# Gate products of tile pairs as seven half-size block products in a two-layer block on one Trainium2 core

## The reference

```python
p = h @ w_in[l]                       # h: 512 token rows (and, in layer one, 256 context rows) x 1024
o_a = global_attention(...)           # 512 features each
o_b = window_attention(...)
o_c = short_conv(...)
g_a, g_b, g_c = jnp.split(jax.nn.sigmoid(p[..., OFF_GATE:]), 3, axis=-1)     # 1024 features each
merged = g_a * (o_a @ w_branch[0]) + g_b * (o_b @ w_branch[1]) + g_c * (o_c @ w_branch[2])
x = x + gt1 * (merged @ w_out)
```

## Time and profile before

| | |
|---|---|
| median of three runs | 3093.0 us (3089.81 to 3094.14) |
| profiled execution | 3090.21 us, span 3088.4 us |
| PE busy | 2977.6 us, 96% of the span |
| DVE, ACT busy | 1051.9 us (34%), 613.1 us (20%) |
| layer one's merge | about 436 to 870 us of the span |
| layer two's merge | about 1895 to 2172 us |
| granted PE clock, mean | 0.995 |

### The profile page before, as it was taken

One profiled execution on the slowest core, in us unless ns is written; L12 is line 12 of the kernel. 1 busy time (PEld: TensorE's weight loads), 2 busy tenths in 40 slices (PEclk: granted clock), 3 DMA queues, 4 the chain that ended last, 5 costly groups with the idle time before them and its releaser, 6 DMA issues.

```text
span 3088.4 us, 32609 instructions
## 1 busy us (share of the span) xinstructions
PE 2977.6 (96%) x13043; PEld 1402.2 (45%) x13043; DVE 1051.9 (34%) x1566; ACT 613.1 (20%) x1121; POOL 75.0 (2%) x88
## 2 busy tenths in 40 slices
PE   7999999999999999999999999999979898899999
PEld 4565655555545222222335555444323222244547
DVE  4754645556514000000157553011120010137352
ACT  3135530000003110111031552000111100021161
POOL 1000000000000010102000000000000000000000
PEclk9999999999999999999999999999999999999999
DMA  8120013534513999999850101222499999963200
GB/s 253 41 83 14 15 52 124 185 137 146 174 41 143 388 369 401 365 401 357 314 157 14 56 20 53 77 67 95 177 355 408 408 408 408 407 206 82 68 1 28
DMA packets 266076, 578.83 MB, mean 187 GB/s; under 512 B 62040, under 2 KB 140136, under 8 KB 265800
## 3 DMA queue, kind: packets, MB, share of 16 engines
q1 hardware_dynamic: 258064, 554.09, 48.9%
q0 software_dynamic: 7552, 22.61, 2.4%
q10 hardware_dynamic: 312, 0.05, 0.0%
HBM read 561.49 MB, written 15.20 MB: 187 GB/s over the span
## 4 chain that ended last, share of the span: by engine, by line
PE 87%; DMA 9%; DVE 2%; issue 1%; ACT 1%; SPq 0%; DVEq 0%; POOL 0%; ACTq 0%; POOLq 0%
PE ps L1026 32%; PE ps L1430 10%; PE ps L1545 6%; PE ps L1042 5%; PE ps L1442 5%; PE ps L1090 5%; PE ps L1258 4%; PE ps L1270 3%; PE ps L1304 3%; PE ps L1103 3%; DMA ring<-in_w_e_down 2%; PE ps L1066 2%; PE ps L1486 2%; DMA ring<-in_w_e_gate 1%; DMA ring<-in_w_e_up 1%; PE ps L1240 1%
## 5 line engine op out<-in xcount | busy, mean ns | idle before, releaser
L1026 PE MATMUL ps<-hT,ring 128*128 128x512 f32 (+1 forms) x2080 | 771.8, 528 | 1.5 <-ACT hT L1772 1.4
L1026 PEld LDWEIGHTS ps<-hT,ring 128*128 128x128 f32 x2080 | 394.4, 190 | 366.1 <-issue 341.7
L1430 PE MATMUL ps<-ring,hT 128*64 128x512 f32 x992 | 234.4, 602 | 3.8 <-DMA ring<-in_w_e_up 3.8
L1042 PE MATMUL ps<-hT,ring 128*128 128x512 f32 (+1 forms) x448 | 181.5, 533 | 0.7 <-DVEq L1757 0.7
L1772 ACT ACTIVATE prob<-ps 128x512 f32<-128x512 f32 (+1 forms) x67 | 46.4, 692 | 681.0 <-PE ps L1026 681.0
L1545 PE MATMUL ps<-ring,hT 128*64 128x512 f32 x640 | 150.4, 603 | 14.9 <-DMA ring<-in_w_e_down 10.6
L1772 ACT ACTIVATE prob<-prob,nms 128x768 f32<-128x768 f32 (+5 forms) x224 | 159.2, 711 | 18.9 <-DVE nms L2395 8.6
L1090 PE MATMUL ps<-merged,ring 128*128 128x512 f32 (+1 forms) x384 | 144.4, 531 | 3.1 <-issue 3.1
L1026 PE MATMUL ps<-obuf,ring 128*128 128x512 f32 (+1 forms) x384 | 143.4, 523 | 0.0
L1270 PE MATMUL ps<-con,prob 128*128 128x128 f32 x872 | 140.2, 283 | 1.3 <-DVE merged L2419 0.5
L1270 PEld LDWEIGHTS ps<-con,prob 128*128 128x128 f32 x872 | 96.4, 140 | 89.5 <-issue 78.8
(11 more groups left out here) (341 smaller groups left out, 3204.0 us busy)
## 6 DMA issues: line engine op xcount, KB each, us to landing
ring<-in_w_e_gate SPq DMA_DIRECT2D x79, 1024.0 KB, 15.8
ring<-in_w_e_up SPq DMA_DIRECT2D x65, 1024.0 KB, 15.0
ring<-in_w_e_down SPq DMA_DIRECT2D x60, 1024.0 KB, 14.6
ring<-in_w_in SPq DMA_DIRECT2D x49, 1024.0 KB, 6.9
ring<-in_w_ada SPq DMA_DIRECT2D x48, 1024.0 KB, 6.8
merged<-in_w_e_up SPq DMA_DIRECT2D x25, 1024.0 KB
merged<-in_w_e_down SPq DMA_DIRECT2D x19, 1024.0 KB
merged<-in_w_e_gate SPq DMA_DIRECT2D x18, 1024.0 KB
```

Of the source, the lines that this page charges most:

```text
L1026: mm = pe.matmul(ps[:, b + a:b + e], lhs[:, k, :], rhs[:, k, a:e], start=k == 0, stop=k == nk - 1)
L1042: mm = pe.matmul(ps[:, BANK[SIDE]:BANK[SIDE] + hi - lo], ring3(slot)[:, k, m % 2 * P:(m % 2 + 1) * P], h3[:, k, lo:hi], start=k == 0, stop ...
L1430: mm = pe.matmul(ps[e * CX:(e + 1) * CX, b + h * 512:b + (h + 1) * 512], lhs, second_weights(slot_of[sub], e, h), start=k == 0, stop=k == ...
```

## The change

For a pair of tiles (256 gate features) the 1024x256 weight chunk and the 1024x512 token columns are each cut in 2 x 2 blocks: two halves of K (0:4, 4:8), two feature tiles, two halves of 256 token columns. The four output blocks come from seven block products (a Strassen-Winograd scheme) in place of eight. All twelve pairs of layer two are done so, and the eight pairs of branches 0 and 1 in layer one; layer one's branch 2 stays as it was, and context columns are multiplied plainly (`context`).

New jobs: `hsum` (DVE: sums of token blocks, once per layer, in place in `h3` too), `wsum` (DVE: sums of weight blocks, one per pair, placed ahead of the branch jobs of the pair before), `gate2` (PE: `seven_products`; ACT and DVE: copy, additions, sigmoids).

```diff
+            def long(j):
+                return {"hsum": 0, "wsum": 0, "gate2": 2}.get(j[0], 1)
...
-            count, passed, share = len(todo), 0, len(jobs) - 4
+            count, passed, share = len(todo), 0, sum(map(long, jobs)) - 4
...
+                if j[0] in ("hsum", "gate2") or j[0] == "branch" and j[2] < 2 and j[3] % 2:
+                    continue
                 while todo and (count - len(todo)) * share < passed * count:
...
+            in_pairs = ((0, 1), (2, 0, 1))[l]
+            pairs = [(l, br, n) for br in in_pairs for n in range(KD // 2)]
...
+            dense += [j for p in pairs[:1] for j in (("hsum", l), ("wsum",) + p)]
+            for at, p in enumerate(pairs):
+                dense += [("gate2",) + p] + [("wsum",) + q for q in pairs[at + 1:at + 2]]
+                dense += [("branch", l, p[1], 2 * p[2] + m) for m in range(2)]
...
+                if j[1:] == PAIR_FIRST[l]:
+                    need(oT_ready, ("O", l, 2 * TILES[l] - 1))
+                    need(token_sums_ready, ("hsum", l))
...
+                times("p1", a, w[:, 0:4, 0:P], h3[:, 0:4, 0:HALF], True)
+                if l == 0:
+                    context(0)
+                need(weight_sums_ready, ("wsum",) + j[1:])
+                times("p6", b, s2, t2, True)
+                times("p5", c, s1, t1, True)
+                if l == 0:
+                    context(1)
+                need(seven_added, j[1:] + ("u2",))
+                times("p7", b, s3, h3[:, 0:4, HALF:NX], False)
+                need(first_product, j[1:])
+                times("p2", a, w[:, 4:8, 0:P], h3[:, 4:8, 0:HALF], False)
+                need(seven_added, j[1:] + ("u3",))
+                times("p4", b, w[:, 4:8, P:2 * P], t4, False)
+                need(seven_added, j[1:] + ("22",))
+                times("p3", c, s4, h3[:, 4:8, HALF:NX], False)
+                chunk_end[cn] = (seven_full.sem, seven_full.at[j[1:] + ("p3",)])
...
+                elif kind == "gate2":
+                    b = BANK[job[j][0]]
+                    if before_pair[j[1:]][1]:
+                        A.need(gate_used, before_pair[j[1:]][1])
+                    A.need(seven_full, j[1:] + ("p1",))
+                    A.do(sc.copy(probT[:, 1, 0:HALF], ps[:, b:b + HALF]), first_product, j[1:])
...
+                    V.do(v.tensor_tensor(t1, b12, b11, ALU.subtract))
+                    V.do(v.tensor_tensor(t2, b22, t1, ALU.subtract))
+                    V.do(v.tensor_tensor(t4, b21, t2, ALU.subtract))
+                    V.do(v.tensor_tensor(b12, b22, b12, ALU.subtract), token_sums_ready, j)
...
+                    if before_pair[j[1:]][0]:
+                        V.need(seven_full, before_pair[j[1:]][0][1:] + ("p3",))
...
+                    V.do(v.tensor_tensor(s1, a21, a22, ALU.add))
+                    V.do(v.tensor_tensor(s2, s1, a11, ALU.subtract))
+                    V.do(v.tensor_tensor(s4, a12, s2, ALU.subtract))
+                    V.do(v.tensor_tensor(s3, a11, a21, ALU.subtract), weight_sums_ready, j)
...
+                    V.need(first_product, j[1:])
+                    V.need(seven_full, j[1:] + ("p6",))
+                    V.do(v.tensor_tensor(c12, p1, second, ALU.add), seven_added, j[1:] + ("u2",))
+                    V.need(seven_full, j[1:] + ("p7",))
+                    V.do(v.tensor_tensor(c22, p1, second, ALU.add), seven_added, j[1:] + ("u3",))
+                    V.do(v.tensor_tensor(c22, c22, third, ALU.add), seven_added, j[1:] + ("22",))
```

More of the change, by code:

```diff
@@ L790, in chunk_of @@
                 return (kind, l, t // 2), t % 2
+            if kind in ("gate2", "wsum"):
+                return ("gate", l, t, j[3]), 0
             if kind == "gate":
@@ L830, in chunk_dmas @@
             return plain(w_out[l], n * CH)
-        WEIGHTED = ("qk", "v", "conv_c", "conv_x", "conv_b", "gate", "branch", "silg", "side", "wout", "wt")
+        WEIGHTED = ("qk", "v", "conv_c", "conv_x", "conv_b", "gate", "gate2", "wsum", "branch", "silg", "side", "wout", "wt")
         def chunk_keys(j):
@@ L1027, in product, with seven_products, times, context @@
                 part(mm, key)
+            def seven_products(j):
+                l = j[1]
+                cn, slot = weights(chunk_of(j)[0])
+                if j[1:] == PAIR_FIRST[l]:
+                    need(oT_ready, ("O", l, 2 * TILES[l] - 1))
+                    need(token_sums_ready, ("hsum", l))
+                a = begin(j)
+                b = a + 512
+                c = begin(j + ("c",), HEAD_SUMS if l == 0 or j[3] % 2 else SIDE)
+                w = ring3(slot)
+                s1, s2, s4, s3 = weight_sums
+                t1, t2, t4 = token_sums[l]
+                def times(name, bank, lhs, rhs, first):
+                    for k in range(4):
+                        mm = pe.matmul(ps[:, bank:bank + HALF], lhs[:, k, :], rhs[:, k, :],
+                                       start=first and k == 0, stop=k == 3, skip_group_check=not first)
+                    mm.then_inc(seven_full.sem, 1)
+                def context(m):
+                    if m == 0:
+                        begin(j + ("x",), SIDE)
+                    o = BANK[SIDE] + m * NC
+                    for k in range(KD):
+                        mm = pe.matmul(ps[:, o:o + NC], w[:, k, m * P:(m + 1) * P], h3[:, k, NX:NT], start=k == 0, stop=k == KD - 1)
+                    if m == 1:
+                        part(mm, j + ("x",))
+                times("p1", a, w[:, 0:4, 0:P], h3[:, 0:4, 0:HALF], True)
[15 more added lines that the diff above has]
+                chunk_end[cn] = (seven_full.sem, seven_full.at[j[1:] + ("p3",)])
             def run(j):
@@ L2300, in run @@
                     g = probT[:, d % 2, 0:w]
-                    V.need(sig_ready, ("gate", l, br, d))
+                    if (l, br, d // 2) in before_pair:
+                        V.need(pair_sigmoid, (l, br, d // 2, "12"))
+                    else:
+                        V.need(sig_ready, ("gate", l, br, d))
                     b = V.read(j)
```

63 lines of the change are left out of this document (59 added, 4 removed).

## The result

The changed kernel takes 3171.7 us (median of 4 runs, 3170.8 to 3175.8) against 3092.1 us (4 runs) for the one before on the same chip: ratio 1.0263, 95% interval 1.0251 to 1.0276. It is 80 us slower; the forecast was 3146 us, with a range of 3126 to 3162. The direction was right, the size missed by 26 us.

The account below looks back on a forecast made before the run. PE was taken to bound both merges, with SP's queue stalling layer one after the change. Layer one +58, clock +10 and layer two -13.5 gave +55 on 3090.2, 3145, stated as 3146 us for the median; range 3126 to 3162.

Parts of the forecast that it names:

- layer one without clock: From layer one's last branch-2 product to its last branch product: 321.0 us against 262.8 before, +58.2.
- low clock, both layers: Lower PE clock behind seven stalls in layer one and one in layer two: 10 us of at most 16.
- layer two without clock: Layer two's 12 pairs: 20.6 us saved, 7.1 us of waits for `hsum` and `wsum` at the start, -13.5.
- stretch between the merges: From layer one's merge to layer two's: no change, since nothing behind the merges absorbs the difference.
- Bound, gain, mechanism: In both merges PE binds; twenty pairs save 34.3 us without waits; layer one's late branch chunks in SP's queue decide.
- Landing ... 2.5 MB land after 9.3, 3.5 MB after 11.9: Layer one's branch chunks behind `w_ada` chunks: PE idle 9.4 us at pairs 1, 2, 5 and 12.0 at 3, 4, 6.
- A stall costs between 0 and 2.0 us more ... I take 10 us: Clock price behind eight stalls, seven in layer one and one in layer two: 10 us taken of at most 16.
- The row for 2.0: Earlier trace: after 12.13 us idle PE runs at 0.50, eight 0.43 us instructions take 5.46, 2.0 us lost.
- The row for 0: Earlier trace, program's start: after 9.24 us idle the clock shows 1.00, read as no loss.
- Products: Both merges: seven products of a pair take 12.00 us, 1.714 each; with layer one's context products 18.86.
- The first, 3108: Rival: layer one's transfers hide and DVE's queue binds, layer one +27 instead of +58, total 3108 us; chance 0.08.
- Worse than the sum: Rival: stalls at the upper landing, all with low clock, 0.25 us more per pair: 3160 us and over; chance 0.12.

Follow-up runs that it names:

- e3: Changed kernel with plain products instead of the seven in layer one's branches 0 and 1, new order of jobs and chunks kept, layer two unchanged: 3169.6 us.
- e1: Changed kernel with each layer-one pair's 0.5 MB branch chunk read directly behind that pair's gate chunk, ahead of the `w_ada` chunks: 3133.0 us.
- e10: Changed kernel with layer one's branch chunk (branches 0 and 1) in one transfer of 128 partitions instead of two of 64: 3165.0 us.
- e6: Changed kernel, but SP issues nothing behind a branch chunk of layer one's branches 0 and 1 until that chunk has landed: 3171.8 us.
- e9: Changed kernel with PE multiplying constants in six layer-one stalls, fills cut to the measured waits: 3161.8 us.
- e2: Changed kernel with seven products in layer two alone; layer one's merge has the earlier kernel's job order and plain products: 3078.6 us.
- e13: Changed kernel with the turn of the three PSUM slots moved on by two ahead of layer one's first w_out product: 3171.9 us.
- e8: Changed kernel with branch chunk ahead, `w_ada` sums moved, layer one's first-pair context products before the sums, three of layer two's `hsum` instructions early: 3085.8 us.
- e5: Changed kernel with PE multiplying 20 to 31 products of constants before the first branch product of six layer-one pairs: 3232.8 us.

## Why the prediction was right in direction and wrong in size

The 80.6 us between the two spans, by the terms of my sum:

| term | forecast | measured |
|---|---|---|
| layer one without clock | +58.2 | +69.6 |
| low clock, both layers | +10 | +21.8 |
| layer two without clock | -13.5 | -13.6 |
| stretch between the merges | 0 | +3.5 |
| rest | 0 | -0.7 |

So the sum was 26 us short: 11.4 in layer one's landings and products, 11.8 in the clock, 3.5 in the stretch between, and 0.8 the other way.

- **Bound, gain, mechanism: right.** Six stalls for `in_w_branch` of 8.8 to 12.7 us, `hsum` 10.7 (forecast 10.4) and 6.1 (5.9), u2 2.0 (2.3), pair 7 2.1. e3 shows that the order of jobs and chunks alone makes the loss, and e1 that 39 us of it hang on the place of the branch chunk. Layer two is right to 0.1 us.
- **"Landing ... 2.5 MB land after 9.3, 3.5 MB after 11.9": too short.** From the end of p3 to PE's start it was 10.5 to 11.8 us at pairs 1, 2 and 5 and 13.4 to 13.7 at the others; with pair 7 the stops sum to 78.4 us where I had 68.4. I scaled the branch chunk's 1.3 us from its size, and it comes in two transfers of 64 partitions: in one, a wait is 1.4 us shorter (e10), and at pair 2 PE starts 9.35 us after the first issue (718.82 to 728.17), where I had 9.4. The Trainium skill's fit (DMA: Bandwidth & Descriptors, Anatomy of one DMA) was for the other path; the estimate by it, 8 us for 2.5 MB, misses the measured 10.2 (e6) by 2.2 us, my own by 0.9.
- **"A stall costs between 0 and 2.0 us more ... I take 10 us": neither end was a bound.** Here 1.5 to 3.1 us were lost behind each of the seven branch stalls (14.4 in all), 2.8 behind each `hsum`, and 1.8 behind the 1.99 us wait for u2: 21.8 us. I had counted eight stalls; pair 7's and u2's short waits make ten. e9 gives 9.9 of it back. Both rows that I read the earlier trace rows say less than I took from them.

  The row for 2.0: the clock was low from PE's return at 2256.27 to about 2261.8. Of these 5.5 us the first 2.0 passed over four products of 16 columns and 0.91 us of idle, so only 3.6 us of low clock fell on dense work. The eight instructions were not all at 0.50 either: at 0.86 us each they would have taken 6.9 us, not 5.46.

```profile
2260.00:2262.00 2.00, 2.00 (x4) 0.88 (x3) 0.00 (x0) 0.00 (x0) 0.96 (x1) 0.55 0.68 158
```

  The row for 0: the clock column says 1.00 at the program's start, but the 42 equal instructions there did not run at one pace. PE was busy throughout, and the first 24 took 5.0 us (0.21 each), the rest about 0.11 each. The windows show 11 of them under way in 2.00 us, then 15 in 1.59:

```profile
16.00:18.00 2.00, 2.00 (x11) 2.00 (x10) 0.77 (x1) 1.64 (x2) 0.00 (x0) 1.00 1.05 410
20.00:22.00 2.00, 1.59 (x15) 1.29 (x12) 1.82 (x3) 1.85 (x3) 0.00 (x0) 1.00 1.01 403
```

  Half pace for 5 us is what a low clock looks like elsewhere. That it was the clock is not shown, but the row is no evidence that idle time costs nothing, and the discount from 16 to 10 us rested on it. A better row stood in the same trace, ahead of layer one's first w_out product: 1.78 us of waiting, then 8.80 us for 16 instructions that take 7.11 at full clock (the second line is e2's).

```profile
872.55 8.80 PE L1090 MATMUL ps<-merged,ring 128*128 128x512 f32 x16 [1.78 <-issue]
873.01 7.11 PE L1176 MATMUL ps<-merged,ring 128*128 128x512 f32 x16 [1.78 <-issue]
```

  The Trainium skill (TensorE: Matmul & The Clock Gate, Why this matters for your kernels) warned of just this, and the trace agrees with it in that every one of these stalls was followed by 0.50; by it I put the time 4 to 6 us above my sum, which was too little as well.
- **Products.** Seven of them take 12.09 us and not 12.00, a pair of layer one with its context products 19.0 to 19.1 and not 18.86; what is left of layer one's difference, 1.4 us, goes to them.
- **The stretch between**, 3.5 us: 2.7 are a wait for a PSUM slot, whose turn is shifted by eight gate jobs fewer; but restoring it gave nothing in the time (e13). Behind that wait two pairs of constant products ran at low clock, 1.81 and 1.41 us in place of 1.02 each. What the merge otherwise leaves behind stays open.
- **The rivals.** The first, 3108, said what is left when the chunks land in time. e1 is that case, and it took 3133: +49 in layer one and not +27. I had taken each of DVE's late items once, but they add up in its queue, four sums in front of a branch tile and an `rsum` behind them, and DVE waits for landings of its own. "Worse than the sum" is what came, at 0.12: both unknown costs stood at or over my upper ends at once. It is not that longer stalls cost more clock: in e10 3.1 us were lost behind the stall of 6.63 us and 1.9 behind that of 11.24. Each was simply too small, and was multiplied by the number of stalls.

## What to carry to other kernels

A change that saves engine time and reorders jobs also reorders the queue that feeds them: write down for each chunk what frees its slot and who stands behind it, before counting products. Price the order by itself (plain products in the new order), for that run shows whether the saving was ever the question. Where a chain of stalls is forecast, take the clock's price from a row where dense work follows the wait at once and goes on until the clock is back, check the clock column against the pace of equal instructions, count the short waits too, and multiply an error per stall by the number of stalls before stating a range.

## What the runs showed of the hardware

- After a wait of about 2 us the granted clock can go to 0.50 or stay. In the changed kernel the products behind the 1.99 us wait for u2 took 3.31 and 2.31 us in place of 1.89 each, and in e8 a product behind a wait of 1.95 us lost nothing:

```profile
667.50 3.31 PE L1081 MATMUL ps<-hT,sq_rs 128*128 128x256 f32 x8 [1.99 <-DVE prob L2427]
633.87 1.99 PE L1084 MATMUL ps<-hT,sq_rs 128*128 128x256 f32 x8 [1.95 <-DVE prob L2438]
```

- Behind each branch stall of 6.6 us or more (changed kernel, e3, e6, e10) the branch product was slower than its 10.48 us, by 1.5 to 3.1 us, and the loss did not grow with the stall.
- Equal instructions at the program's start ran at 0.21 us each for 5 us and at 0.11 after that, while the clock column said 1.00 for both.
- 0.5 MB in one transfer of 128 partitions instead of two of 64 came 1.4 us earlier behind the same 2 or 3 MB.
- PE multiplying constants while it would wait kept the granted clock at 1.00 (all of 757 to 781 us in e9) and made the kernel 9.9 us faster (e9); with fills twice as long as the waits it was 61 us slower (e5).
